# Keys of the decode attention: turned by VectorE in 32x32 blocks and multiplied by sixteen 32x32 tiles of TensorE

## The reference

```
q5 = q.reshape(B, Tq, KV_HEADS, HPG, dh) * (dh ** -0.5)
s = jnp.einsum('bqgjd,bgqnkd->bgjqnk', q5, kg)      # selected keys, 1024 a sequence
...
s = jnp.einsum('bqgjd,bkgd->bgjqk', q5, kw)         # window keys, 512 a sequence
mw = (kpos[None, :] <= qpos[:, None]) & (kpos[None, :] > qpos[:, None] - WINDOW) & (kpos[None, :] >= 0)
p = masked_softmax(s, mw[None, None, None])
o_win = jnp.einsum('bgjqk,bkgd->bqgjd', p.astype(vw.dtype), vw)
```

## Time and profile before

| | |
|---|---|
| median of the runs | 589.01 us |
| the profiled execution: time, span | 592.85 us, 591.1 us |
| TensorE (PE) busy | 560.5 us, 95% of the span |
| VectorE (DVE) busy | 335.8 us, 57% |
| ScalarE (ACT) busy | 266.2 us, 45% |
| chain that ended last | PE 60% of the span; DVE 5%, ACT 2% |
| mean granted clock of TensorE | 0.981 |

### The profile page before, as it was taken

One profiled execution on the slowest core, in us unless ns is written; L12 is line 12 of the kernel. 1 busy time (PEld: TensorE's weight loads), 2 busy tenths in 40 slices (PEclk: granted clock), 3 DMA queues, 4 the chain that ended last, 5 costly groups with the idle time before them and its releaser, 6 DMA issues.

```text
span 591.1 us, 12729 instructions
## 1 busy us (share of the span) xinstructions
PE 560.5 (95%) x5102; PEld 505.4 (85%) x5102; DVE 335.8 (57%) x830; ACT 266.2 (45%) x601; POOL 135.2 (23%) x237
## 2 busy tenths in 40 slices
PE   6899999999988999998899999999999999999994
PEld 4899999989977899797689787676778999999994
DVE  5633222488748665336327548858766257773465
ACT  5434435444413352433233267767777253223333
POOL 0016323121101121460330005556453300000000
PEclk9899999999969999999999999999999999999998
DMA  9437722553227234492382215755355533415103
GB/s 300 167 93 220 255 73 71 213 175 128 78 68 243 82 92 123 144 333 95 96 296 72 69 41 142 192 149 143 92 151 134 149 110 108 144 37 176 42 8 145
DMA packets 59468, 80.51 MB, mean 136 GB/s; under 512 B 7249, under 2 KB 48145, under 8 KB 59154
## 3 DMA queue, kind: packets, MB, share of 16 engines
q1 hardware_dynamic: 48320, 49.44, 26.9%
q0 software_dynamic: 10368, 29.14, 15.8%
q10 hardware_dynamic: 722, 1.12, 0.5%
HBM read 65.23 MB, written 8.13 MB: 124 GB/s over the span
## 4 chain that ended last, share of the span: by engine, by line
PE 60%; DVE 5%; ACT 2%; issue 1%; ACTq 0%; DVEq 0%
PE m L1698 40%; PE s L2005 4%; PE o L2012 3%; PE t L1907 1%; PE s L1880 1%; PE s L1881 1%; PE s L1883 1%; PE o L1966 1%; PE t L1844 1%; PE s L1921 1%; PE m L1782 1%; PE o L1992 1%; PE t L1985 1%; DVE w_lo L1272 1%; PE t L1978 1%
## 5 line engine op out<-in xcount | busy, mean ns | idle before, releaser
L1698 PE MATMUL m<-h_hi,w_hi 128*128 128x272 f32 x448 | 134.0, 299 | 0.5 <-DVE w_lo L1272 0.5
L1698 PE MATMUL m<-h_hi,w_lo 128*128 128x272 f32 x448 | 129.2, 288 | 0.0
L1698 PE MATMUL m<-h_lo,w_hi 128*128 128x272 f32 x448 | 128.8, 287 | 0.0
L1698 PE MATMUL m<-w_hi,h_hi 128*128 128x256 f32 (+2 forms) x360 | 105.4, 293 | 2.8 <-issue 1.9
L1698 PE MATMUL m<-w_lo,h_hi 128*128 128x256 f32 (+2 forms) x360 | 102.8, 286 | 0.0
L1698 PE MATMUL m<-w_hi,h_lo 128*128 128x256 f32 (+2 forms) x360 | 102.8, 286 | 0.0
L1272 DVE TENSOR_TENSOR w_lo<-raw,w_hi 128x1024 fp32r<-128x1024 f32 (+2 forms) x62 | 71.1, 1154 | 42.9 <-ACT w_hi L1003 42.9
L1698 PEld LDWEIGHTS m<-h_hi,w_hi 128*128 128x128 f32 x448 | 84.2, 188 | 12.3 <-issue 10.9
L1698 PEld LDWEIGHTS m<-h_lo,w_hi 128*128 128x128 f32 x448 | 84.5, 189 | 0.0
L1698 PEld LDWEIGHTS m<-h_hi,w_lo 128*128 128x128 f32 x448 | 84.5, 189 | 0.0
L955 POOL DMA_DIRECT2D U<-p_turn x108 | 58.1, 546 | 102.7 <-DVE p_turn L1604 94.8
(11 more groups left out here) (296 smaller groups left out, 961.3 us busy)
## 6 DMA issues: line engine op xcount, KB each, us to landing
raw<-in_w_in SPq DMA_DIRECT2D x36, 512.0 KB, 3.8
U<-in_x_p SPq DMA_DIRECT2D x8, 512.0 KB, 5.4
raw<-in_w_o SPq DMA_DIRECT2D x8, 512.0 KB, 3.7
U<-p_turn POOLq DMA_DIRECT2D x54, 64.0 KB, 2.5
U<-p_turn SPq DMA_DIRECT2D x42, 64.0 KB, 2.9
raw<-in_w_in SPq DMA_DIRECT2D x8, 256.0 KB, 3.2
U<-in_ck_win POOLq DMA_DIRECT2D x8, 256.0 KB, 3.2
U<-in_cv_win POOLq DMA_DIRECT2D x8, 256.0 KB, 6.3
```

Source lines behind the costliest of these rows:

```text
L1698: ins = mm(out, lhs(a, k), rhs(b, k), start=(k == 0 and a + b == 0), stop=(k == n - 1 and a == 1))
```

## The change

- `kt` has no part on TensorE, and none on ScalarE. VectorE turns a gathered buffer at once, from SBUF to SBUF, with one `transpose` of 128x512, which turns each 32x32 block where it lies: in a block of partitions 32a.. the 32 key numbers (index f) lie on partitions and 32 key rows along them. The buffer goes back to the ring when this is done. There are two sets of turned keys, `key_blocks[0]` and `[1]`, used by turns.
- `qkS` of a chunk has 64 matmuls in place of 4: for each quarter f of the 128 numbers, each sequence b and each partition strip a, a 32x32 weight by 128 keys. Strip a and column strip b address one of the 16 tiles of the array; strip a writes bank a of four, so that the scores of a chunk lie in a quarter of each of four banks (`by_chunk`). The four f add up in place. The banks `s0`, `s1`, `s2` and `o` are now one tensor `so`.
- The weights need each quarter of the queries on each strip: 16 small DMAs on the sync queue copy `q_bd` to `q_quarters`, at step `("xt", 2, 0)`.
- `s_mask` reads the selected scores as four pieces of 128x256 in place of two of 128x512.
- `s_pv` is cut in two, `s_pt` and `s_pv`, with a `main` tile between them, and in round 0 one more before `s_out`. The turning of a chunk is put a step or more ahead of its product; both first products of round 1 follow one another after `s_out` of round 0. The number of `main` tiles from the last `hidl` to the prompt's attention stays 19.

```diff
@@ plan() @@
+    def keys(q, c):
+        order.extend(("kt", q, c, b) for b in range(QB))
+
+    keys(0, 0)
     main(1)
     order += [("mix", u1[3]), ("kc", NCH - 1)]
+    main(1)
+    keys(0, 1)
+    order += [("qkS", 0, 0)]
+    main(1)
+    keys(0, 2)
+    order += [("qkS", 0, 1)]
+    main(1)
+    order += [("qkS", 0, 2)]
     for q in range(NQ):
-        for c in range(3):
-            order += [("kt", q, c, b) for b in range(QB)]
-            main(AFTER_KEYS[c])
-            order += [("qkS", q, c)]
         for n, step in enumerate(("s_max", "s_turn", "s_imp", "s_mask", "s_exp", "s_scale")):
...
             order += [(step, q)]
-            main(AFTER_STEP[q][n])
-        order += [("s_pv", q), ("s_out", q)]
+            if q == 0 and n in (1, 3):
+                keys(1, n // 2)
+            main(1)
+        order += [("s_pt", q)]
+        main(1)
+        order += [("s_pv", q)]
+        if q == 0:
+            main(1)
+        order += [("s_out", q)]
+        if q == 0:
+            order += [("qkS", 1, 0), ("qkS", 1, 1)]
+            keys(1, 2)
+            order += [("qkS", 1, 2)]
@@ sync @@
+                elif s == ("xt", 2, 0):
+                    wait_evacuated(sp, T_AT[("qTs",)])
+                    for f in range(4):
+                        for a in range(4):
+                            sp.dma_start(q_quarters[32 * a:32 * a + 32, f, :, :], q_bd[32 * f:32 * f + 32, :, :]).then_inc(q_spread, 16)
@@ gpsimd, load_key @@
-                pool.wait_ge(t_done, key_freed(n))
+                if n < KEY_RING:
+                    pool.wait_ge(t_done, key_freed(n))
+                else:
+                    pool.wait_ge(key_turned, n - KEY_RING + 1)
@@ vector @@
-                elif kind == "kt" and t_uses(s) == ["dve"]:
+                elif kind == "kt":
...
+                    dve.wait_ge(key_loaded[ld % KEY_RING], 16 * (ld // KEY_RING + 1))
+                    if b == 0:
+                        if n >= 2:
+                            dve.wait_ge(qk_done, n - 1)
...
+                    v.transpose(key_blocks[n % 2][b], key_ring[:, ld % KEY_RING, :]).then_inc(key_turned, 1)
@@ tensor @@
-                    for b in range(QB):
-                        ins = mm(S[c][32 * b:32 * b + 32, :], q_bd[:, QB * q + b, :], keysT[:, b, :], start=True, stop=True)
+                    for f in range(4):
+                        for b in range(QB):
+                            for a in range(4):
+                                r = slice(32 * a, 32 * a + 32)
+                                keys = key_blocks[n % 2][b].rearrange("p (m f i) -> p f m i", m=4, f=4)
+                                ins = mm(by_chunk[32 * b:32 * b + 32, chunk_at[c], a, :], q_quarters[r, f, QB * q + b, :], keys[r, f, :, :],
+                                         start=(f == 0), stop=(f == 3), skip_group_check=True)
```

More of the change, by code:

```diff
@@ L413, in t_uses @@
         return ["dve"]
[L414 to L417, removed]
+    if kind in ("s_pt", "s_pv"):
+        return ["dve", "act"]
     if kind == "ct":
@@ L454, in key_freed @@
 def key_freed(n):
-    return load_turned(len(LOADS) - RING + n // 2) if n < KEY_RING else T_AT[KEYS[n - KEY_RING]] + 1
+    return load_turned(len(LOADS) - RING + n // 2)
 def raw_count(r):
@@ L576, in nsa_gmlp_layer @@
         vw = U[:, 4096:6144].rearrange("p (b s d) -> p b s d", b=QB, s=4)
-        keysT = U[:, 6144:8192].rearrange("p (b n) -> p b n", b=QB)
-        ptr = [U[:, 7680:8192], U[:, 12928:13440]]
+        ptr = [pm("b_sp"), U[:, 12928:13440]]
+        q_quarters = prm[:, 0:1024].rearrange("p (f b n) -> p f b n", f=4, b=NB)
+        turned_late = placed("turned_late", 3072, [P, 1024])
+        key_blocks = [[U[:, 6144 + 512 * b:6656 + 512 * b] for b in range(QB)],
+                      [x[:, 512 * b:512 * b + 512] for x in (prm[:, 1024:2048], turned_late) for b in range(2)]]
         pts = U[:, 13440:13824]
@@ L601, in nsa_gmlp_layer @@
         xr = [xr_slots[:, 4, :]] + [sig_flat[:, n * T:n * T + 1024] for n in (11, 13, 0)] + [xr_slots[:, 3, :]]
-        bank = [ctx.enter_context(nc.psum_tensor(n, [P, 512], F32)) for n in ("m0", "m1", "t0", "t1", "s0", "s1", "s2", "o")]
-        M, TB, S, O = bank[0:2], bank[2:4], bank[4:7], bank[7]
+        bank = [ctx.enter_context(nc.psum_tensor(n, [P, 512], F32)) for n in ("m0", "m1", "t0", "t1")]
+        SO = ctx.enter_context(nc.psum_tensor("so", [P, 2048], F32))
+        M, TB, S, O = bank[0:2], bank[2:4], [SO[:, 512 * n:512 * n + 512] for n in range(3)], SO[:, 1536:2048]
+        by_chunk = SO[:, :].rearrange("p (a c n) -> p c a n", a=4, c=4)
+        chunk_at = (1, 2, 3)
         x_loaded = [sem(f"x_loaded{n}") for n in range(NT + 1)]
@@ L1150, in _ @@
                                          scale=SCALE, accum_out=st[:, 50:51]).then_inc(s_exp, 1)
[L1151 to L1157, removed]
+                elif kind in ("s_pt", "s_pv"):
+                    act.wait_ge(t_done, t + 2)
+                    if kind == "s_pv":
+                        act.wait_ge(pv_part, 2 * s[1] + 1)
+                    nc.scalar.copy(ptr[1], TB[(t + 1) % 2][:, :]).then_inc(t_act, 1)
                 elif kind == "cx":
@@ L1927, in _ @@
                                 ins = mm(O[32 * b:32 * b + 32, 64 + 32 * y:96 + 32 * y], q_bd[:, QB * q + b, :], k_newT[:, y, :],
-                                         start=True, stop=True)
+                                         start=True, stop=True, skip_group_check=True)
                     ins.then_inc(qk_done, 1)
```

97 lines of the change are left out of this document (42 added, 55 removed).

## The result

| | before | after |
|---|---|---|
| median of the runs | 588.78 us (588.38 to 590.21, 4 runs) | 601.38 us (599.74 to 602.32, 4 runs) |
| ratio | | 1.0206, 95% interval 1.0177 to 1.0236 |
| profiled execution, span | 592.85 us, 591.1 | 599.74 us, 597.9 |
| TensorE, VectorE, ScalarE busy | 560.5, 335.8, 266.2 us | 559.7, 344.9, 257.4 us |

The kernel became 12.6 us slower; the forecast was 580.3 us, 8.5 us faster. The two profiled executions differ by 6.9 us only: that of before was 4.1 us above the median of these runs, that of after is the fastest of its four. The prompt's attention begins at 340.32 us, for 333.50, and is as long as before.

What follows compares the result with a forecast made beforehand. TensorE was taken as the bound, busy 560.5 of 591.1 us. 15.1 + 3.5 - 8.4 - 1.5 = 8.7 us saved gave 584.1 profiled, 580.3 us as median; own range 577.3 to 583.5, wider range 576.5 to 589.0.

Steps and rivals of the forecast that it cites:

- What the new products cost: Six products of queries by keys: 128 passes each on 16 tiles side by side, 1.0 us a product, no change.
- half of it: Rival at the six products: only eight tiles at once, 1.75 + 0.1 us a product, 583.3 us; chance 0.12.
- far bound of 3.5 us a product: Rival at the six products: partition strips take turns, 32 rounds, 3.5 us each, 591.2 us in all; chance 0.13.
- test of 7.5 ns a pass: Products' issue rate: 16 passes of 32 columns within 0.31 us gave 7.5 ns each, against a skill rule of 25 ns.
- Turning removed: Key turning on TensorE: 96 transposes and the idle time before them go, 15.1 us saved.
- Weights by values: Weights-by-values step of both rounds: main tiles cover waits, 8.99 to 6.1 us and 7.19 to 6.6, 3.5 saved.
- VectorE's waits: Four places where TensorE waits for VectorE, which now turns the keys: cost 8.4 us together.
- ZB0: First main tile of ZB0: TensorE waits 3.0 us for VectorE, 0.5 before; cost 2.5 us.
- Round 1's scaling: Turning of round 1's weights: VectorE has more work before `s_scale`, with as many tiles on TensorE; cost 1.8 us.
- (0,2): Product of key chunk 2 in round 0: VectorE needs 7.7 us against TensorE's 7.4; wait 0.4 us.
- (1,2): Last product of round 1: TensorE idles from 5.4 us until VectorE's turns end at 9.1; cost 3.7 us, the largest.
- Clock: The new waits of 3.0 and 3.7 us cause one fall to the lower clock; cost 1.5 us.

Runs made afterwards that it cites:

- the kernel with eight tiles: Changed kernel, with the last three feature quarters of each product made for two of four pages, so 8 tiles work instead of 16; 590.3 us, one run.
- the run of this step alone: Kernel before, with only weights by values split in two around a main tile taken from each round's second chunk; 591.44 us, ratio 1.0029.
- With traffic and order mended: Changed kernel with main tiles between round 1's products, value loads and round 1's key loads held behind products, keys of round 1 turned later; 579.80 us, ratio to before 0.9833.

## Why the prediction was wrong

**The step that failed** is "What the new products cost": "I take 1.0 us, no change". Measured 1.83 us undisturbed and 3.9 on the mean, 17.9 us more in all. The prediction had none for the products and 4.1 for waits in front of two of them.
- Six times 1.83 for 5.76 us is 5.2 us more: the rival "half of it" (forecast 1.85 us, chance 0.12). The argument for sixteen tiles came from rows that show two tiles side by side by rows and four by columns, never both. Shown by the kernel with eight tiles beside the changed one: 13.6 and 13.9 ns a pass.
- The other 12.6 us, and most of the 1.0 in the small products, are pauses and the lower clock in and behind them. No rival named them. The prediction counted the 128 passes and asked how fast they can start; it did not ask how fast 256 instructions can be brought. Its far bound of 3.5 us a product bought the right size by a wrong mechanism: strips that take turns would have made the first product slow too.
- Its test of 7.5 ns a pass from 16 small passes was too short a run: in the changed kernel the first 32 passes of a product do start 7.6 ns apart, and from the 65th to the 113th they start 13.9 ns apart. The 25 ns that it held against this is not seen either.

The sum came out 18.7 us off (+10.0 for -8.7): 13.8 us by the products beyond their forecast of +4.1, 4.5 by the waits and the clock around the main tiles and the prompt's scores, 1.0 by the small products, and the weights by values gave 0.6 more than forecast.

**Turning removed**, -15.1: right to 0.1.

**Weights by values**, -3.5: 16.19 to 12.11, -4.1. Right in kind. But the run of this step alone shows that it is worth nothing or less: the main tile has to come from somewhere. In the change it came from round 1's products, which it left in a row.

**VectorE's waits**, 8.4 us. ZB0: forecast 3.0, measured 3.08, right. Round 1's scaling: forecast 1.8 more; measured 1.38 - 0.28 and 1.0 at the prompt's scores, 2.1, right in size. The run of the split alone has much the same waits there (1.36 and 0.66) without any key turned on VectorE, so they come with the new order of the main tiles. (0,2) did not wait. (1,2), the largest at 3.7, never appeared: VectorE ended the keys' turning at 301.38 us while TensorE was still waiting for code until 303.61, in the middle of (1,1). So it was hidden behind a longer wait; this run does not show what it would have cost with fast products. Missed: 2.86 us ahead of `s_out`. The prediction credited the main tile there with covering 0.50 us and did not follow VectorE's program order, in which reading that tile's sums comes first.

**Clock**, one fall of 1.5 us forecast: there were four stretches at the lower level between 252 and 307 us, 17 us long together. Each fell in or behind a pause or a wait. Before had one of 3.4 us in its stretch.

**The rest.** `ps` was to begin near 325 us; it began at 340.32, in an execution that was 3.2 us ahead when it came to the changed stretch; its length is unchanged as forecast. The copies of the queries cost nothing, as forecast. Of the 12.6 us between the medians the changed stretch explains 10.0; the rest lies between executions of the same kernel, and no run here takes it apart.

With traffic and order mended the same change gives 579.8 us. That this is near the forecast of 580.3 is chance: its products took 11.6 us where 5.8 and 4.1 of waits were forecast, and its other waits cost less.

## What to carry to other kernels

Count TensorE's instructions in every dense stretch, not its passes or columns only: a run of more than some 80 small matrix products and weight loads can break into pieces beside DMA traffic (here a product of 1.83 us took up to 7.28), and several blocks of 256 instructions in a row can need more time than they execute in. Put wide matrix products between the dense ones, and loads that aren't urgent behind them. When a step is moved to cover a wait, write down in which order the reading engine now works: the tile that covers one engine's wait is that engine's next task.

## What the hardware showed unexpectedly

- 32x32 tiles: passes of 128 columns start 13.9 ns apart with 16 tiles and 13.6 with 8; passes of 32 or 64 columns no closer than 9.6 to 9.9 ns over a whole product.
- Code reaches TensorE in packets of 16 KB, 256 instructions. In a row of dense products without traffic a block came every 3.45 us; TensorE resumes 1.2 to 1.5 us after a packet's end. Some packets start 3.5 to 4.1 us after the block ahead was begun, all of them beside traffic of GpSimd's DMA queue; beside the hardware queue alone at a share of 0.99 one started after 1.3 us.
- Beside DMA traffic a dense run of instructions can break into bursts of 8 to 12 with 0.4 to 0.7 us between them, after its first 80 or so; as much traffic left all runs of 64 alone, and some of 160 and 256.
